# The extra expert units stand between the third and the fourth expert of the sweep, not behind its end

## What is computed

```python
N_EXPERTS = 64; TOP_K = 6; EXPERT_DIM = 256; SHARED_DIM = 256; EXPERT_BLOCK = 128

def swiglu(x, w1, w3, w2):
    return (jax.nn.silu(x @ w1) * (x @ w3)) @ w2

# moe_ffn: router, top 6 of 64 experts per token, then
padded = (counts + EXPERT_BLOCK - 1) // EXPERT_BLOCK * EXPERT_BLOCK   # blocks of 128 rows
yg = lax.map(expert_block, (xg, blk_e)).reshape(P, D) * slot_w[:, None]
routed = jax.ops.segment_sum(yg, slot_tok, num_segments=T + 1)[:T]
return routed + swiglu(xs, sh_w1, sh_w3, sh_w2)
```

## Time and profile before

| | us |
|---|---|
| median of 3 runs | 2142.55 |
| the runs | 2142.55, 2143.75, 2138.14 |
| the profiled execution | 2141.59 |
| its span | 2139.7 |
| TensorE busy | 1851.8 (87%) |
| VectorE busy | 859.7 (40%) |
| ScalarE busy | 461.4 (22%) |
| POOL busy | 368.3 (17%) |
| weight loads on SP's queue, all | 499.70 MB |

### The profile page before, as it was taken

The page is one execution under the profiler, slowest core; times in us unless marked ns, Lnnn a source line. Parts: engine busy times, 40 slices in busy tenths (PEclk is TensorE's granted clock), DMA queues, the critical chain, the costliest instruction groups (busy, mean ns, idle before and its releaser), DMA issues.

```text
span 2139.7 us, 30541 instructions
## 1 busy us (share of the span) xinstructions
PE 1851.8 (87%) x9472; PEld 965.5 (45%) x9473; DVE 859.7 (40%) x1527; ACT 461.4 (22%) x823; POOL 368.3 (17%) x563
## 2 busy tenths in 40 slices
PE   6989999885998878887999899776888899988996
PEld 3455555433544444444444443344444444444543
DVE  1545656556312222222115499576222212222226
ACT  4144444211111111101110565220111011111112
POOL 0010000001111111111104288002111111111113
PEclk9999999997999999999999999887999999999997
DMA  9488011357999999999997202256999999999955
GB/s 409 170 350 318 1 40 40 122 197 293 365 419 392 402 399 388 404 401 393 374 371 266 109 1 118 78 229 268 396 408 406 393 390 408 384 398 404 397 185 202
DMA packets 95248, 625.10 MB, mean 292 GB/s; under 512 B 16080, under 2 KB 16208, under 8 KB 56912
## 3 DMA queue, kind: packets, MB, share of 16 engines
q1 hardware_dynamic: 44208, 499.70, 58.1%
q0 software_dynamic: 26112, 79.72, 10.1%
q10 hardware_dynamic: 24864, 44.84, 5.8%
HBM read 563.38 MB, written 76.28 MB: 299 GB/s over the span
## 4 chain that ended last, share of the span: by engine, by line
PE 57%; DMA 22%; DVE 10%; issue 4%; POOL 3%; ACT 3%; SPq 0%; POOLq 0%; ACTq 0%; DVEq 0%
DMA ring<-in 21%; PE PS L1063 11%; PE PS L1057 9%; PE PS L1070 5%; PE PS L1084 4%; PE PS L1095 4%; PE PS L1285 3%; PE PS L1048 3%; PE PS L985 3%; POOL work L612 3%; PE PS L1039 2%; PE PS L948 2%; PE PS L1003 2%; PE PS L1013 2%; PE PS L1232 2%
## 5 line engine op out<-in xcount | busy, mean ns | idle before, releaser
L1063 PE MATMUL PS<-ring,work 128*64 128x256 f32 x3360 | 415.9, 404 | 120.2 <-issue 119.9
L1063 PEld LDWEIGHTS PS<-ring,work 128*64 128x64 f32 x3360 | 246.7, 145 | 265.5 <-issue 169.3
L1456 DVE TENSOR_TENSOR work<-work,PS 64x256 f32<-64x256 f32 x105 | 44.4, 423 | 525.5 <-ACT work L665 524.5
L1057 PE MATMUL PS<-ring,work 128*128 128x512 f32 x400 | 185.7, 619 | 21.5 <-issue 12.3
L1070 PE MATMUL PS<-ring,work 128*64 128x512 f32 x840 | 203.3, 605 | 1.0 <-DVE work L1468 1.0
L1462 DVE COPY work<-PS 128x1024 f32<-128x1024 f32 x128 | 156.8, 1225 | 13.7 <-PE PS L1095 9.8
L532 POOL COPY col_i<-idx 128x1 int32 (+1 forms) x128 | 23.4, 182 | 797.5 <-PE PS L1095 790.1
L538 POOL DMA_INDIRECT work<-h_rows,col_i x128 | 125.4, 979 | 165.4 <-issue 165.4
L665 ACT ACTIVATE work<-PS 64x256 f32<-64x256 f32 x105 | 39.5, 376 | 522.2 <-PE PS L1063 519.9
L1095 PE MATMUL PS<-cst,work 128*128 128x128 f32 x1040 | 142.5, 280 | 10.7 <-DMA work<-h_rows,col_i 10.7
L1095 PEld LDWEIGHTS PS<-cst,work 128*128 128x128 f32 x1040 | 114.9, 142 | 63.8 <-issue 52.8
(11 more groups left out here) (247 smaller groups left out, 2141.5 us busy)
## 6 DMA issues: line engine op xcount, KB each, us to landing
ring<-in SPq DMA_DIRECT2D x156, 2048.0 KB, 17.3
ring<-in SPq DMA_DIRECT2D x132, 1024.0 KB, 18.0
y_rows<-sq POOLq DMA_DIRECT2D x2, 14336.0 KB, 58.0
y_rows<-work ACTq DMA_DIRECT2D x210, 128.0 KB
ring<-in SPq DMA_DIRECT2D x3, 4096.0 KB, 14.0
y_rows<-work ACTq DMA_DIRECT2D x46, 256.0 KB
ring<-in SPq DMA_DIRECT2D x2, 3072.0 KB, 14.3
work<-in SPq DMA_DIRECT2D x2, 2048.0 KB, 16.9
```

The source lines that it names most:

```text
L1057: last = mm(bank(6), lhs(c), w13(s)[:, :, c, :], start=(c == 0), stop=(c == DC - 1))
L1063: last = mm(bank(6)[64 * q:64 * q + 64, 0:F], lhs(c)[:, 0:64], w13(s)[:, q, c, :], start=(c == 0), stop=(c == DC - 1), tile_position=(0, 6 ...
```

## The change

The extra units leave the end and stand between units 2 and 3 on every engine. They get buffers of their own, in the parts of the accumulator `acc` that nothing uses during the sweep. Their weights go into the ring's fourth slot before any other expert's do: SP waits for the number of extra units (`unit_rdy`), then loads them where it loaded expert 3. Expert 3 takes the slot of expert 0, once that expert's up products are done. With u the expert, the ring's slots are (2, 3, 0) for the first three and (2, 3, 0, 1) in turn from expert 3 on, and expert 6 is the first to use slot 1 behind the extra unit, after the up products of expert 3. The wait for each refill is the same distance as before from expert 7 on. Each down product but the last of a layer gets one more wait, for the silu of the following expert (`gate_rdy`). The first load of `pw1` of the convolution module is asked for one expert earlier.

The diff, cut to its core:

```diff
+        unit_x, unit_xT, unit_y = acc[:, 0, :], acc[:, 1, :].rearrange("p (c t) -> p c t", c=DC), acc[:, 3, :]
-        SHARED, EXTRA = 3, 2
+        SHARED, EXTRA = 3, 1
         def slot_of(u):
-            return (3, 2, 0, 1)[u % RING]
+            return (2, 3, 0)[u] if u < 3 else (2, 3, 0, 1)[(u - 3) % RING]
...
-                for u in range(RING):
+                for u in range(3):
                     if i == 0 and u == 2:
                         sp.wait_ge(wo_ps, DC)
-                    if u == RING - 1:
-                        sp.wait_ge(hd_out, 64 * (i + 1))
                     expert(ds(u, 1), slot_of(u), w_in[slot_of(u)])
+                sp.wait_ge(hd_out, 64 * (i + 1))
                 sp.wait_ge(unit_rdy, i + 1)
-                sp.wait_ge(m["dn_ps"], E - 2)
                 many = nc.sync.value_load(unit_i[0:1, XMAX:XMAX + 1], min_val=0, max_val=XMAX)
...
+                refill_up(3, slot_of(3), 1)
+                refill_up(4, slot_of(4), 2)
+                refill_down(3, slot_of(3), 1)
+                refill_up(5, slot_of(5), 3)
+                refill_down(4, slot_of(4), 2)
+                refill_up(6, slot_of(6), 4)
+                refill_down(5, slot_of(5), 3)
+                expert_down(ds(6, 1), slot_of(6), w_in[slot_of(6)])
+                refill_up(7, slot_of(7), 4)
...
             def down(w, par, s, big, final=False):
                 pe.wait_ge(m["actT_ev"], w + 1)
+                if not final:
+                    pe.wait_ge(gate_rdy, w + 2 + i * E)
                 pe.wait_ge(m["y_ev"], w)
...
             unit(2, slot_of(2), slot_of(1), 32, 32, 0)
+            many = nc.tensor.value_load(unit_i[0:1, XMAX:XMAX + 1], min_val=0, max_val=XMAX)
+            with nc.tensor.If(many > 0):
+                pe.wait_ge(xgT_ev, 4 + i * E)
+                with nc.tensor.Fori(0, many) as j:
...
+            for u in range(3, 7):
+                unit(u, slot_of(u), slot_of(u - 1), 32 * loads_of(u), 16 * ((u + 1) // 2 + 1), u % 2)
```

More of the change, by code:

```diff
@@ L324, in build @@
         J_CTX, J_X, J_FFN0, J_MIX1, J_LN, J_FFN1, J_FIN = range(7)
-        SHARED, EXTRA = 3, 2
+        SHARED, EXTRA = 3, 1
         CHUNK_BANK = (3, 0, 1, 2, 4, 5, 6, 7)
         def slot_of(u):
-            return (3, 2, 0, 1)[u % RING]
+            return (2, 3, 0)[u] if u < 3 else (2, 3, 0, 1)[(u - 3) % RING]
         def loads_of(u):
-            return u // RING + 1
-        LOADS = E // RING
+            return 1 if u < 3 else (u - 3) // RING + (1 if slot_of(u) == EXTRA else 2)
+        LOADS = [sum(slot_of(u) == n for u in range(E)) for n in range(RING)]
         ROW_BANK = [n % 2 for n in range(4)]
@@ L460, in load_moe, with refill_up, refill_down @@
                         expert(ds(e, 1), EXTRA, m["t_w"])
+                def refill_up(u, s, w):
+                    sp.wait_ge(m["up_ps"], w)
+                    expert_up(ds(u, 1), s, w_in[s])
+                def refill_down(u, s, w):
+                    sp.wait_ge(m["dn_ps"], w)
+                    expert_down(ds(u, 1), s, w_in[s])
+                refill_up(3, slot_of(3), 1)
[7 more added lines that the diff above has]
+                refill_up(7, slot_of(7), 4)
+                with nc.sync.Fori(0, (E - 8) // 4) as g:
+                    for r in range(4):
+                        refill_up(g * 4 + (8 + r), slot_of(8 + r), g * 4 + (5 + r))
+                        refill_down(g * 4 + (7 + r), slot_of(7 + r), g * 4 + (4 + r))
+                sp.wait_ge(m["up_ps"], E - 3)
+                sp.dma_start(slot_ap(SHARED)[:, 0:UP], sh_w[i][:, 0:UP]).then_inc(sh_in, 16)
+                refill_down(E - 1, slot_of(E - 1), E - 4)
+                sp.wait_ge(m["dn_ps"], E - 3)
+                sp.dma_start(slot_ap(SHARED)[:, UP:SLOT], sh_w[i][:, UP:SLOT]).then_inc(sh_in, 16)
             for n in range(MODBUF):
@@ L548, in moe @@
                 gather(1, 1, xg_in[1])
[L549 to L553, removed]
+                for u in range(2, 4):
+                    pool.wait_ge(xgT_ps, u - 1 + i * E)
+                    gather(u, u % 2, xg_in[u % 2])
                 pool.wait_ge(unit_rdy, i + 1)
@@ L718, in moe @@
                 shared_silu(0)
[L719 to L732, removed]
                 shared_silu(1)
@@ L1171, in expert_in @@
                     pe.wait_ge(xgT_ev, u + 1 + i * E)
-                    pe.wait_ge(w_in[slot], n_w + i * 32 * LOADS)
+                    pe.wait_ge(w_in[slot], n_w + i * 32 * LOADS[slot])
                     either(u, lambda big: up(u, lambda c: xgT[par][:, c, :], slot, big))
```

134 lines of the change are left out of this document (66 added, 68 removed).

## The result

The changed kernel takes 2149.07 us (median of 8 runs, 2144.84 to 2156.27), the kernel before 2138.94 us (8 runs, 2136.07 to 2146.83): a ratio of 1.0043, 95% interval 1.0032 to 1.0054. It is slower by 0.43%, and the forecast was 2150. The profiled execution of the changed kernel was the fastest of its eight, with a span of 2142.9 us against 2139.7. Much of the study is about why these two differ, so the document reads both.

The account below looks back on a forecast made before the run. It took TensorE to bound the sweep's start, weight loads the rest, and TensorE with the gathered sum the layer ends. Start loss 43.8 plus wait 1.3 minus end gain 38 gave +7.1 us, so 2150, range 2137 to 2160.

Parts of the forecast that it names:

- the new wait: Wait on gate_rdy: free in the sweep, 0.65 us before the last unit's down products, 1.3 us for both layers.
- What the end gains: End of a layer without the extra unit: between 15 and 20.5 us, taken as 19 a layer, 38 in all.
- the prediction's own sign: End of a layer: the prediction is wrong if it gains less than 17 us.
- When the extra rows come: Before the extra unit: gathered rows land at 552.8 and 1494.7 us, so TensorE waits 2.3 and 3.8 us.
- The price behind such a wait: Extra unit after TensorE idled for its rows: slower matmuls between clock levels, 0.8 and 1.6 us added.
- the gather is in time: Rival, extra unit: rows land before unit 2 ends, so it costs 15.0 us; sum -1.4, 2141 us; chance 0.13.
- S: How much later unit 8 starts, kept to the sweep's end: 19.3 and 24.5 us, 43.8 together.
- the third and fourth step: Start of sweep: DMA engines idle from near 556 us until up 6; from there 39.5 us to unit 8.
- The second step: Layer 0's start: the extra unit's load comes later beside the first gather, so everything there starts 2.5 us earlier.
- The end gives only TensorE's own time: Rival, layer ends: gathered sums bind, so the gain is 15 us a layer; sum +15, 2158 us; chance 0.17.
- The loads catch up: Rival, sweep start: 14 idle us don't matter, unit 8 11.5 and 16.8 us later; sum -8.4, 2134; chance 0.09.
- Only the bytes count: Rival, sweep: the extra unit hides under loads, costing one expert's 9.6 us a layer; -17.5, 2125 us; chance 0.04.

Follow-up runs that it names:

- `after_none`: The changed kernel with the extra unit's load, gather, products and store left out in both layers; ratio 0.9913 to the kernel before.
- `before_none`: The kernel before with the extra unit's load, gather, products and store left out in both layers; ratio 0.9861 to the kernel before.
- `pw1late`: The changed kernel with both loads of pw1 asked for one expert later; ratio 1.0091 to the kernel before.
- `again`: The changed kernel itself run once more, for a second profile (span 2155.0 us); ratio 1.0035 to the kernel before.
- `up6early`: The changed kernel, with SP asking for expert 6's weights as soon as the extra unit has used its slot; ratio 0.9997 to the kernel before.
- at 6/7: The changed kernel with the extra unit between units 6 and 7, its weights as the eighth expert of the ring; ratio 0.9959 to the kernel before.

## Why the prediction was right, and where it was not

**The total** was forecast at 2150 and is 2149.07, the sum at +7.1 us where the medians say +10.1. A hit as near as that is luck, twice over. The forecast was built on a median of 2142.55 for the kernel before, whose eight runs then gave 2138.94. And both large terms were too large: in the first profile the starts lose 37.6 us in A and C, where 43.8 and 1.3 for the new wait were forecast, and the ends give 34.4 instead of 38, which makes +3.2. In the second it is 46.5 and 31.3, +15.2. The forecast lies between two executions of the same program.

**What the end gains**, forecast 19 us a layer, is 14.0 and 20.4 in the first profile, 12.9 and 18.4 in the second, together 34.4 and 31.3 instead of 38. The mechanism was right in both layers: POOL starts sooner, the sum follows. In layer 1 the size was too: the gathers start 20.2 us earlier against the first shared group, as the 20 I put in. In layer 0 the same step is the one that failed, and by the prediction's own sign (an end that gains less than 17 us) it was wrong there. I had POOL start 20 us earlier and the first sum 16; the trace has 13.0 and 13.1 (the first sum at 1142.48, 17.7 us behind 1124.82, against 30.7 before). What I left out is that `pw1` stands beside the last stores, and that these are what the gathers wait for once the unit is gone. With its second load behind the gathers B is 50.6, near layer 1's 48.4 to 50.4. I had only looked at its being asked for earlier and set that at zero; it gains 4.5 us (B of `after_none` against `before_none`). The shared down products took 15.62 us where I took 13.8.

**When the extra rows come**, forecast 2.3 and 3.8 us after TensorE is ready, depends on the execution. In layer 0 it is nothing or 2.79 to 3.84 us, in layer 1 never more than 0.83 us, less than forecast. The price behind such a wait, the up products at the lower clock, I put at 0.8 us in layer 0, where it is 1.5 to 3.1 (8.59 in `pw1late`, 10.20 in `again`, against 7.13), and at 1.6 in layer 1, where it is 1.7 (8.83 against 7.13) behind only 0.36 idle in the first profile and nothing behind the same 0.36 in `up6early`. The rival "the gather is in time" is what the first profile shows in layer 0, and its 2141 stands beside that run's 2144.84; but its S of 16.2 and 19.1 and its 38 us at the ends are not what that profile has.

**The loads** went as the third and fourth step say. The DMA engines are idle from about 557 until up 6, asked for at 567.62 and 1513.89 (forecast 570.0 and 1515.2, with the waits). From there to unit 8 it is 40.7 and 41.1 us (forecast 39.5, bounds 37 to 41.5). The second step, everything 2.5 us earlier in layer 0, was 1.7 us (unit 2 ends at 548.76). Unit 8 starts at 608.33 and 1554.94 (forecast 609.5 and 1554.7), so S is 18.2 instead of 19.3 in layer 0. S for layer 1 must not count what layer 0 carries over (3.0 us), so it is 21.7 instead of 24.5, and the 1554.7 was hit by that carry. One reading was off without harm: in layer 0 unit 7 is already idle for 2.13 us before it starts at 581.07 in the kernel before, so unit 8 is not the first. What I had not seen is that the slot itself has a price, 5.3 us in A and 9.1 in C with nothing loaded into it; in my steps it was hidden in the count of loads behind up 6.

**The new wait** was put at 0.65 us a layer. Ahead of the last but one down products TensorE is idle for 0.52 us in either layer, where the kernel before has no idle time:

```profile
1120.13 1.94 PE L1076 MATMUL PS<-ring,work 128*64 128x512 f32 x8 [0.52 <-issue]
...
2065.51 1.94 PE L1076 MATMUL PS<-ring,work 128*64 128x512 f32 x8 [0.52 <-issue]
```

**The rivals.** "The end gives only TensorE's own time" comes near the size for layer 0 (13 to 14 us against 15), but not by its mechanism: the gathers bind there because they start late, not by POOL's pace or the six buffers. For layer 1 it is wrong. "The loads catch up" is out: unit 8 comes where the count of bytes puts it. "Only the bytes count" is wrong for this place and nearly right for the other: at 6/7 it cost 9.5 and 10.9 us, and with `pw1` out of the way the kernel takes 2127.92 us, where that rival said 2125. The rule of the Trainium skill (page "Perfetto Trace Analysis", section "Optimization Strategy") says that interleaving regimes may improve performance. The trace agrees where the moved work lands in the stretch in which loads bind (0.9959), and not at the start of the sweep, where they don't (1.0043).

**A version that beats both kernels** is `pos7_pwend`: the unit between units 6 and 7 and the second load of `pw1` behind the gathers, 0.9936 (0.9921 to 0.9951).

## What to carry to other kernels

Work that is to hide under loads belongs behind the point from which loads bind, and its buffer should come out of the ring in turn. A slot taken from the first prefetch costs that prefetch even when nothing is loaded into it, and a long stretch of TensorE work put where the ring is full leaves the DMA engines idle until a slot comes free. When a tail gets shorter, look at which transfers now run beside the one that everybody waits for; here the load of later weights took back a third of the gain of a layer (14.0 us where the other layer has 20.4).

## What the runs showed of the hardware

A store of 128 KB took 14.2 us beside loads of 3 MB each (15.8 in `pw1late`) and 4.2 us as they ended, though it is issued on another queue. A gather of few rows issued between 542.8 and 544.5 us, at a DMA share of 0.96 to 1.05, landed in time for 549 in three profiles and 3 to 4 us late in three others, each issued 4.4 us behind the load ahead of it. And a wait of 2.79 to 3.84 us in front of 16 large matmuls was followed by 8.6 to 10.2 us for them instead of 7.13, at a granted clock of 0.50 to 0.66 from 555 to 560 us, so these three waits cost 1.6 to 1.9 times themselves.
